# Two DRAM table broadcasts issued later, a rows' quarter converted ahead of a weight half, and another order of routing, shared expert and expert loads

## The reference, cut to what matters

```python
mod = silu(c) @ w_ada + b_ada                      # six vectors of 1024
h = rms_norm(x, norm1_g) * (1 + scale1) + shift1
proj = h @ w_in                                    # 1024 x 5120
...                                                # two attentions, branches, w_out
h2 = rms_norm(x, norm2_g) * (1 + scale2) + shift2
scores = sigmoid(h2 @ w_router)                    # 64 experts in 8 groups
choice = scores + router_bias
# sum of the top 2 of each group -> best 4 groups -> best 8 experts of those
wts = scores[chosen] / sum(scores[chosen]) * 2.5
routed = sum over chosen e of wts_e * (silu(h2 @ w_gate_e) * (h2 @ w_up_e)) @ w_down_e
y = routed + (silu(h2 @ w_gate_sh) * (h2 @ w_up_sh)) @ w_down_sh     # shared expert
x = x + gate2 * y
```

## Time and profile before

| | us |
|---|---|
| median of three runs | 1350.07 |
| the profiled execution, its own time | 1351.17 |
| its span in the trace | 1349.4 |
| TensorE busy | 1214.6 (90%) |
| VectorE busy | 554.2 (41%) |
| ScalarE busy | 452.0 (33%) |
| first projection matmul starts | 48.33 |
| expert turns, first to last gate and up | 315.97 to 786.24 |
| TensorE idle before expert weights | 41.6, in 7 waits |

### The profile page before, as it was taken

One profiled execution on the slowest core, in us unless ns is written; L12 is line 12 of the kernel. 1 busy time (PEld: TensorE's weight loads), 2 busy tenths in 40 slices (PEclk: granted clock), 3 DMA queues, 4 the chain that ended last, 5 costly groups with the idle time before them and its releaser, 6 DMA issues.

```text
span 1349.4 us, 16311 instructions
## 1 busy us (share of the span) xinstructions
PE 1214.6 (90%) x6501; PEld 841.4 (62%) x6504; DVE 554.2 (41%) x805; ACT 452.0 (33%) x657; POOL 45.6 (3%) x66
## 2 busy tenths in 40 slices
PE   3799999879799789969999869999989988899998
PEld 0677677765344335424554328888879866688886
DVE  0545545674111112211121146464456654544444
ACT  1345445242111112201222134444445544444443
POOL 1000000000000000000000020020010001000000
PEclk9799999979899889979999979999999978899999
DMA  9986565548999999999999996555525106355540
GB/s 345 374 292 241 217 222 185 209 165 331 376 422 420 393 422 421 421 387 422 421 421 421 417 331 196 187 187 187 198 100 187 63 1 210 122 199 189 187 152 32
DMA packets 115087, 360.03 MB, mean 267 GB/s; under 512 B 14995, under 2 KB 62404, under 8 KB 83980
## 3 DMA queue, kind: packets, MB, share of 16 engines
q1 hardware_dynamic: 113360, 352.71, 69.1%
q10 hardware_dynamic: 1340, 2.94, 0.6%
q0 software_dynamic: 320, 3.46, 0.6%
HBM read 355.89 MB, written 4.50 MB: 267 GB/s over the span
## 4 chain that ended last, share of the span: by engine, by line
PE 80%; DMA 9%; DVE 5%; ACT 3%; issue 1%; POOL 1%; SPq 1%; ACTq 0%; DVEq 0%; POOLq 0%
PE bank L1943 30%; PE bank L2120 16%; PE bank L2047 9%; DMA ring<-in_w_up_e 6%; PE bank L2145 5%; PE bank L1994 5%; PE bank L2097 3%; PE bank L2157 3%; DMA att<-in_buckets 1%; PE bank L2212 1%; DMA raw_g<-in_w_in 1%; PE bank L1959 1%; PE bank L2234 1%; DVE g_lo L1243 1%; PE bank L2036 1%
## 5 line engine op out<-in xcount | busy, mean ns | idle before, releaser
L1243 DVE TENSOR_TENSOR g_lo<-raw_g,g_hi 128x2048 fp32r<-128x2048 f32 (+2 forms) x88 | 201.8, 2295 | 119.1 <-ACT g_hi L798 62.4
L2120 PE MATMUL bank<-ring,xg 128*64 128x512 f32 (+1 forms) x1152 | 211.9, 636 | 41.6 <-DMA ring<-in_w_up_e 41.6
L1943 PE MATMUL bank<-g_hi,xt_hi 128*128 128x512 f32 (+1 forms) x592 | 240.1, 406 | 5.8 <-DVE xt_lo L1859 2.2
L1943 PE MATMUL bank<-g_hi,xt_lo 128*128 128x512 f32 (+1 forms) x592 | 232.7, 393 | 0.0
L1943 PE MATMUL bank<-g_lo,xt_hi 128*128 128x512 f32 (+1 forms) x592 | 232.4, 392 | 0.0
L2120 PEld LDWEIGHTS bank<-ring,xg 128*64 128x64 f32 (+1 forms) x1152 | 65.6, 133 | 184.5 <-issue 184.5
L1943 PEld LDWEIGHTS bank<-g_hi,xt_hi 128*128 128x128 f32 x592 | 113.0, 191 | 35.7 <-issue 10.2
L1943 PEld LDWEIGHTS bank<-g_hi,xt_lo 128*128 128x128 f32 x592 | 112.6, 190 | 24.1
L1943 PEld LDWEIGHTS bank<-g_lo,xt_hi 128*128 128x128 f32 x592 | 112.9, 191 | 21.2
L2145 PE MATMUL bank<-ring,a_t 128*64 128x512 f32 (+1 forms) x576 | 102.2, 597 | 1.4 <-DVE pickT L1346 0.9
L1388 DVE SCALAR_TENSOR_TENSOR arena<-arena,w_row_of,bank 128x256 f32<-128x256 f32 x28 | 13.5, 481 | 218.4 <-ACT arena L918 214.3
(11 more groups left out here) (347 smaller groups left out, 1579.9 us busy)
## 6 DMA issues: line engine op xcount, KB each, us to landing
ring<-in_w_gate_e SPq DMA_DIRECT2D x64, 1024.0 KB, 12.5
ring<-in_w_up_e SPq DMA_DIRECT2D x64, 1024.0 KB, 16.5
ring<-in_w_down_e SPq DMA_DIRECT2D x64, 1024.0 KB, 15.5
raw_g<-in_ffn_w_gu SPq DMA_DIRECT2D x44, 1024.0 KB, 8.5
raw_g<-in_w_in SPq DMA_DIRECT2D x26, 1024.0 KB, 7.0
raw_d<-in_ffn_w_down SPq DMA_DIRECT2D x22, 1024.0 KB, 4.9
ada_d<-in_w_ada SPq DMA_DIRECT2D x16, 1024.0 KB, 5.0
raw_g<-in_w_out SPq DMA_DIRECT2D x8, 1024.0 KB, 5.1
```

Of the source, the lines that this page charges most:

```text
L1243: dve.tensor_tensor(lo, raw, hi.bitcast(F32), ALU.subtract).then_inc(S.lo_g, 1)
L1943: last = pe.matmul(out_, src[s][:, c, b * P:(b + 1) * P], w((g_hi, g_lo)[m], i), start=start and i == 0 and k == 0, stop=stop and i == len ...
L2120: last = pe.matmul(bank(4)[r, :].rearrange("p (g n) -> p g n", g=2), xg[:, s // 2 % 2, c, at_:at_ + r.stop - r.start], gate_up_raw(pair, j ...
```

## The change

Four edits.

1. **Tables.** POOL issues the broadcast of `t_dram` only after VectorE's low part of the first `w_in` tile is done, and that of `n_dram` only after the low part of the last `w_in` tile.
2. **Head.** VectorE converts quarter 0 of `xt_lo`, then weight half 0, then quarters 1 to 3.
3. **Routing and shared expert.** `lo_down` runs ahead of the expert selection; the two token blocks' selections are interleaved step by step; `tok_rest` is in halves between the placing steps; the rows to gather have tiles of their own, and `xg` lies where `xt_hi` and `xt_lo` were. TensorE does the shared gate and up in pieces (`shared_rows`) with the counts after 30 of its 48 matmuls, the running sums after 36 and the order after 48. The transposes of the gated rows stand behind the four fills, and the shared down product behind gate and up of turn 0. Two matmuls of totals (L2515, L2516) are gone.
4. **Loads.** SP waits for the shared down product only before the first ordered down load. The list `LOADS` puts gate and up of load 2 ahead of down of load 1. Each expert number is loaded just before its two transfers, behind the wait for the slot.

```diff
+def load_order():
+    loads = []
+    for _, places, load, _, _ in TURNS[1:]:
+        pairs = range(load, load + len(places) // 2)
+        loads += [("gate_up", p, None) for p in pairs]
+        loads += [("down", p, j) for p in pairs for j in range(2)]
+    second = loads.index(("gate_up", 2, None))
+    loads.insert(1, loads.pop(second))
+    return loads
...
                 if load >= 2:
                     sp.wait_ge(used_gu, 4 * (TURN_OF[load - 2] + 1))
-                for g, n in enumerate(("w_gate_e", "w_up_e")):
-                    for j in range(2):
+                for j in range(2):
+                    expert = pair(j)
+                    for g, n in enumerate(("w_gate_e", "w_up_e")):
...
             sp.wait_ge(M.used_g, 2 * G_SH + 2)
-            sp.wait_ge(M.used_d, D_SH + 2)
             sp.wait_ge(ordered, 1)
-            for _, places, load, _, _ in TURNS[1:]:
-                ids = [sp.value_load(order_i[0:1, i:i + 1], min_val=0, max_val=E - 1) for i in places]
...
+            for what, load, j in LOADS:
+                if what == "gate_up":
+                    load_gate_up(load, lambda j: ordered_expert(load, j))
+                else:
+                    if load == 1:
+                        sp.wait_ge(M.used_d, D_SH + 2)
+                    load_down_of(load, j, ids[load, j])
...
+            pool.wait_ge(in_["t1"], 16)
+            pool.wait_ge(M.lo_g, 2 * G_WIN + 2)
             pool.dma_start(t_dram, t_one.unsqueeze(0).to_broadcast([P, NH, BX])).then_inc(in_["tw"], 16)
             pool.wait_ge(in_["n1"], 16)
+            pool.wait_ge(M.lo_g, 2 * (G_WIN + N_WIN - 1) + 2)
             pool.dma_start(n_dram, n_one.unsqueeze(0).to_broadcast([64, NH, NR])).then_inc(in_["nw"], 16)
...
+            transposed(0, qs=(0,))
             split_lo(G_WIN, 0)
-            transposed(0)
+            transposed(0, qs=(1, 2, 3))
...
+            lo_down(D_SH)
...
-            link(route(0))
-            route(1).then_inc(rt_sel, 1)
-            lo_down(D_SH)
-            gate(M, 0, 0)
+            for step in (choice, tops, group_sums, group_max, group_taken, group_in, group_penalty, masked_choice, expert_max,
+                         expert_taken, expert_in, taken_scores, score_sum, score_inverse):
+                both(step)
+            weights(0)
+            weights(1).then_inc(rt_sel, 1)
...
+            tok_rest(0, 0)
...
+            tok_rest(1, 0)
             dve.wait_ge(rt_pos, 3)
...
             pick_rows(0)
-            tok_rest(1).then_inc(tok_lo, 1)
+            tok_rest(1, 1).then_inc(tok_lo, 1)
+            gate(M, 0, 0)
...
+            pe.wait_ge(M.lo_g, 2 * G_SH + 1)
+            shared_rows(0, 0, 0, 4)
+            shared_rows(1, 0, 0, 4).then_inc(M.used_g, 1)
+            pe.wait_ge(M.lo_g, 2 * G_SH + 2)
+            shared_rows(0, 1, 0, 2)
+            counts()
+            shared_rows(0, 1, 2, 2)
+            running()
+            shared_rows(1, 1, 0, 4).then_inc(M.used_g, 1)
+            in_places()
             sparse_phase()
...
                     rows_gate_up(s)
+                    if s == 0:
+                        pe.wait_ge(M.at_lo, D_SH + 1)
+                        pick_t(0)
+                        for b in range(TB):
+                            down(M, D_SH, b)
...
                 for n in range(4):
+                    if n == 2:
+                        pe.wait_ge(M.gated, 2)
                     fill(n)
-                pe.wait_ge(xg_first, 4)
-                pick_t(0)
+                pe.wait_ge(xg_rest, 1)
+                turn(M, 0)
```

More of the change, by code:

```diff
@@ L612, in _, with ordered_expert @@
             sp.wait_ge(M.lo_g, 2 * G_SH + 2)
-            load_gate_up(0, (0, 1))
+            load_gate_up(0, lambda j: j)
             sp.wait_ge(M.lo_d, D_SH + 1)
-            load_pair_down(0, (0, 1))
+            for j in range(2):
+                load_down_of(0, j, j)
             sp.wait_ge(M.used_g, 2 * G_SH + 2)
-            sp.wait_ge(M.used_d, D_SH + 2)
             sp.wait_ge(ordered, 1)
-            for _, places, load, _, _ in TURNS[1:]:
-                ids = [sp.value_load(order_i[0:1, i:i + 1], min_val=0, max_val=E - 1) for i in places]
[L621 to L624, removed]
+            ids = {}
+            def ordered_expert(load, j):
+                turn = TURN_OF[load]
+                i = TURNS[turn][1][2 * (load - TURNS[turn][2]) + j]
+                ids[load, j] = sp.value_load(order_i[0:1, i:i + 1], min_val=0, max_val=E - 1)
+                return ids[load, j]
+            for what, load, j in LOADS:
[5 more added lines that the diff above has]
+                    load_down_of(load, j, ids[load, j])
             def over():
@@ L1673, in _, with tmp, small_tmp, scores @@
-            link(route(0))
-            route(1).then_inc(rt_sel, 1)
-            lo_down(D_SH)
-            gate(M, 0, 0)
+            def tmp(b, i, n=E):
+                t = area(28, 6 * E) if b else rt[:, 2 * E:8 * E]
+                return t[:, i * E:i * E + n]
+            def small_tmp(b, i, at_, n):
+                return tmp(b, i)[:, at_:at_ + n]
+            def scores(b):
+                return bank(7)[:, T + b * E:T + (b + 1) * E]
+            def both(step):
+                for b in range(TB):
+                    ins = step(b)
+                link(ins)
@@ L2532, in _, with shared_rows, counts @@
-            pe.matmul(bank(6)[:, 0:P], by_expert[:, P:2 * P], place[:, :], start=True, stop=True).then_inc(rt_pos, 1)
-            down(M, D_SH, 1)
+            def shared_rows(b, u, c0, n):
+                return rows(bank(4 + b), b, range(4 * u + c0, 4 * u + c0 + n),
+                            lambda t, i: t[:, u, (c0 + i) * 512:(c0 + i + 1) * 512], 512, u == 0 and c0 == 0, u == 1 and c0 + n == 4)
+            def counts():
+                pe.wait_ge(rt_sel, 1)
+                pe.matmul(bank(7)[:, 0:E], before, rt[:, 8 * E:9 * E], start=True, stop=True)
+                pe.matmul(bank(7)[:, E:2 * E], before, rt[:, 9 * E:10 * E], start=True, stop=False)
+                pe.matmul(bank(7)[:, E:2 * E], ones[:, :], rt[:, 8 * E:9 * E], start=False, stop=True)
+                for r in halves:
+                    for b in range(TB):
+                        last = pe.matmul(bank(7)[r, 192:193], rt[:, (8 + b) * E:(9 + b) * E], ones[:, 0:1], start=b == 0, stop=b == 1)
+                last.then_inc(rt_pos, 1)
@@ new lines, in running @@
+            def running():
+                pe.wait_ge(rt_sel, 2)
+                for r in halves:
+                    pe.matmul(bank(7)[r, 193:195], before[low, low], od[low, 2:4], start=True, stop=True)
+                pe.matmul(bank(7)[:, 195:197], ones[low, :], od[low, 2:4], start=True, stop=True)
+                pe.transpose(bank(6)[:, 0:P], rows_in[:, :, :].rearrange("p b e -> p (b e)"), ident)
+                pe.transpose(bank(6)[:, P:2 * P], rt[:, 10 * E:12 * E], ident).then_inc(rt_pos, 1)
```

171 lines of the change are left out of this document (82 added, 89 removed).

## The result

The changed kernel takes 1354.34 us (median of 20 runs, 1352.4 to 1360.67); the kernel before, timed beside it on the same chips, 1350.34 (20 runs, 1348.17 to 1355.73). The ratio is **1.0027, with a 95% interval of 1.0017 to 1.0036**: slower by 3.7 us, between 2.3 and 4.9. The forecast was 1353.3, 3.25 us slower. The profiled execution of the changed kernel took 1354.90 with a span of 1353.1, 3.7 us more than the span of before, so the two profiles differ by as much as the medians do.

A forecast was written before the change was run, and what follows sets the result against it. TensorE, busy for 90% of the span, was taken as the bound, so time counts where it waits or its work shrinks. Terms -0.4 + 0.6 + 2.05 + 1.0 = +3.25 us on the 1350.07 median gave 1353.3 us, range 1349.0 to 1356.5.

The forecast's parts named there:

- Tables and head: Kernel start: moved broadcasts and reordered conversion start the projection 0.6 us earlier, at 47.7; -0.4 us in time.
- VectorE's end at 43.03 does not wait for a transfer: Head: VectorE's adding of the second block's shift, until 43.03, was held independent of transfers; argument against a larger gain.
- Routing: Shared expert to turn 1's gate and up: old waits and two matmuls gone, new waits added; sum +0.6 us.
- Clock in the fills: Fills after the 2.6 us idle for `tok_lo`: half clock might lose 1.7 us; taken as +1.0 us.
- Late register loads: Expert turns: a number's load between slot release and first transfer costs 0.55 us where it counts; +2.05 us in all.
- It counts only where the hop is a chain: turns 3, 9 and 16: Expert turns: delay from slot release to first transfer costs +1.65 us there; turn 2 +0.3, turn 27 +0.1.
- Turns 8 and 15 are bandwidth and take nothing: Later Q turns: their weight waits are bound by transfer bandwidth, so the register loads add nothing there.
- What the earlier weights bring: Expert loads: load 1 issued 7 us earlier is worth nothing from turn 2 on, since load 3 waits for turn 1.
- The lead: Rival: expert phase bound by bytes throughout, so it ends 7.1 us earlier with load 1; 1343.2 us, chance 0.06.
- Hidden loads: Rival: register loads lie under a transfer backlog (0 to 1 us), clock stays up; 1350.8 us, chance 0.27.
- larger head gain: Rival: first `w_in` half's 3.8 us earlier landing reaches TensorE in full; 1349.9 us, chance 0.07.
- worse contention: Rival: the order's VectorE chain takes 1 to 2 us longer, TensorE idles 4 us, clock drops; 1356 us, chance 0.15.

The follow-up runs named there:

- three reads: Changed kernel with every expert number read three times behind the wait for the slot instead of once: ratio 1.0061 to the kernel before.
- late reads: Expert numbers read behind the wait for the slot; as the only edit to the kernel before, ratio 1.0028, median 1354.66 us.
- the zeros: Zero matmuls in seven TensorE waits for expert weights: changed kernel 0.9983, the same reading expert numbers before the wait 0.9964, kernel before 0.9970.
- early reads: Changed kernel with both expert numbers of a pair read before the wait for the slot, as in the kernel before: ratio 0.9993, median 1349.94 us.

## Why the prediction was right, and where it was not

The sum was +3.25 us, the result +3.7, well inside the range, and the late register loads, its largest term, are what makes the change slower. Term by term it was less right than that, and that the total came so near is partly luck: the terms for routing and clock in the fills came out 1.4 to 1.5 us too high together, and the loads cost more, by the medians, than their term.

- **Tables and head, -0.4.** The step was right where its condition holds: at the same clock ahead of it, the projection starts 0.6 us earlier, at 47.7. The first `w_in` half landed before 39.2, since ScalarE split it then without a wait; 37.8 was forecast. In the time, by the ratio, both edits together are worth +0.8 us (-1.1 to +2.7), so neither the 0.4 nor its absence is shown. What I left out is the 16 matmuls behind the wait for `ada_g`: they took 1.1 to 1.7 us more where that wait was 3.1 us or longer than where it was 2.9 or shorter, in every profile, with the edits and without. They stand ahead of VectorE's chain too, so "VectorE's end at 43.03 does not wait for a transfer" was not so: the sums it works on come from these matmuls, which waited for `ada_g` until 32.42.
- **Routing, +0.6.** Measured +0.1 to +0.2. The interleaved selection took 6.2 us for the 6.4 forecast, and `order_i` stood at 301.4, 14.6 us behind the start of the shared expert, where the forecast had 15.0. The counts were waited for 0.2 us, not 0.6, and `tok_lo` 2.41, not 2.6.
- **Clock in the fills, +1.0.** Measured zero: the step that took an idle of 2.6 us as "of the kind that precedes a lower clock" failed. After the idle of 2.41 us the fills ran at full clock:

```profile
303.80:307.90 4.10, 4.10 (x34) 4.10 (x35) 2.25 (x7) 1.87 (x5) 0.00 (x0) 1.00 0.89 360
```

  One row of a drop behind an idle of 2 us was no ground to expect it in another place. That very idle, 2.06 us at 137 to 139 us, is in all 14 profiles, and the clock fell behind it in two; in the eight profiles with the idle of 2.41 us ahead of the fills it fell once, with three reads.
- **Late register loads, +2.05.** The price of one was right (0.56 read by read, 0.59 per hop). The places were not. "It counts only where the hop is a chain: turns 3, 9 and 16" took the turn behind a Q turn for the end of the chain. But turns 8, 15 and 27 start a fixed amount of bytes behind the end of the last Q turn's gate and up, so a hop there is paid once and carried through, and what turns 3, 9 and 16 do in between doesn't matter. "Turns 8 and 15 are bandwidth and take nothing" is true of their own hops and false of what they inherit. By luck both counts come to about four: 2.1 to 2.8 was measured in the intervals. In the medians the late reads cost 3.8 (1.9 to 5.8) and 4.6 (2.5 to 6.7), one of them above my upper end of 3.9. What is on top of the hops was smaller with the zeros, and the profiles with late reads have more half clock in the gate-and-ups behind the waits. So the missing term is most likely a clock term there, and not in the fills where I had put it; that is argued, not shown.
- **What the earlier weights bring, nothing.** Right: turn 2 starts at the release of load 3 plus the transfer, at 348.6, and the DMA engines idle for 3.4 us from 314 and for 4.4 from 333. That moving the shared down product could have delayed SP's second load by 7 us, and that the new order of the loads is there to mend it, the forecast did not see.
- **The rivals.** The lead did not carry; load 3 stayed behind 335.2 us. Hidden loads would have left the ratio at 1.000 with the reads late; it was 1.0028. The larger head gain did not come (ratios 1.0006 and 1.0004), nor did the worse contention: the idle ahead of the fills is 2.41 us, not 4. The Trainium skill's 600 ns for a `tensor_load` ("DMA: Bandwidth & Descriptors", "Latency and other measured facts") would have put a hop at 1.1 us; the 0.79 measured, with 0.27 for the load itself, decide against it here.

What stays open: how much of the late reads' 3.8 to 4.6 us is hop and how much is clock. The share of the clock is argued from one profile each and from the runs with zeros, whose intervals (0.0016 each way) are as wide as the effect. The 1.5 us lost behind ffn2's start in the two profiles belongs to a longer stretch at half clock there (10.2 us for 6.8), which the kernels with early reads have at 6.8 or at 10.2.

## What to carry to other kernels

An instruction put between "slot free" and "transfer issued" cost its time here (0.6 us) at each of the four places where the transfers run dry, and probably what the longer wait does to TensorE's clock; read indices before the wait, where the queue has nothing to do. To find how often a hop counts, look for the gaps in the DMA engines' activity and count those, not the waits of TensorE: all turns up to the next gap inherit the same delay. And where TensorE waits for some microseconds again and again, work that keeps it busy through the wait can give back more than a new order of the work does, until the transfers are the bound.

## What the runs showed of the hardware that I had not expected

- Products of zeros, thrown away, made the kernel faster by 0.3 to 0.4%: 17 to 31 matmuls per wait, some 0.22 us each, kept gate and up of turns 2, 8 and 15 at 2.4 GHz with early reads, 7.07 us instead of 8.6 to 10.0 without zeros.
- An idle of 2.41 us left the clock up in the changed kernel; behind one of 2.06 it was down at 140 us in the profile of before, and not in that of the change. Kernels with the same instructions in a stretch get their half clock there in different places (44.4 and 47.8 us of the 498 between 300 and 798 in the kernel before and in those with the head's edits alone), and two executions can differ by 1 to 2 us before the first changed line (the shared expert starts at 288.23 in the profile of before and at 287.08 and 286.56 in two others with the same code up to there).
- Across the branch, with the register load of its condition, TensorE stood for 7.86 us from the last product ahead of it to the first behind it, and for 3.2 with the zeros ahead of it; under the wait of 9.8 us for `h_tok`, in the other kernels, it doesn't show.
